# A hybrid diffusion backbone: the order of ScalarE's roots and copies in the modulation stage, and the place where the last modulation rows are stored

## The reference

```python
for i in range(DEPTH):                       # 2 layers
    mod_l = split(silu(c) @ ada_w[i] + ada_b[i], 6)       # for the latent tokens
    mod_c = split(silu(c_ctx) @ ada_w[i] + ada_b[i], 6)   # for the context tokens
    hl = rmsnorm(xl, norm_g[i, 0]) * (1 + sc1) + sh1
    hc = rmsnorm(xc, norm_g[i, 0]) * (1 + csc1) + csh1
    # layer 0: neighbourhood attention (q, k, v of 16 heads); layer 1: recurrent block
    xl = xl + gt1 * mixer_l;  xc = xc + cgt1 * mixer_c
    xl, xc = ... + gate2 * hier_moe(modulated rmsnorm of each)
out = rmsnorm(xl, final_g)
```

## Time and profile before

| | |
|---|---|
| median of 3 runs | 3079.86 us |
| lowest, highest | 3075.73, 3080.54 us |
| profiled execution | 3072.01 us |
| its span, first to last instruction | 3070.2 us |
| TensorE matmul busy | 2621.4 us (85%) |
| ScalarE, VectorE, GpSimd busy | 929.2, 1092.5, 420.1 us |
| mean granted TensorE clock | 0.929 |
| modulation stage | 0 to 197 us |

### The profile page before, as it was taken

One profiled execution on the slowest core, in us unless ns is written; L12 is line 12 of the kernel. 1 busy time (PEld: TensorE's weight loads), 2 busy tenths in 40 slices (PEclk: granted clock), 3 DMA queues, 4 the chain that ended last, 5 costly groups with the idle time before them and its releaser, 6 DMA issues. The chain is left out here.

```text
span 3070.2 us, 68426 instructions
## 1 busy us (share of the span) xinstructions
PE 2621.4 (85%) x27112; PEld 1748.1 (57%) x27113; DVE 1092.5 (36%) x2328; ACT 929.2 (30%) x2036; POOL 420.1 (14%) x628
## 2 busy tenths in 40 slices
PE   5779999999969959999999169999869599999980
PEld 1457777777735546666666134444335466666650
DVE  3423333333334432222222755556543322222226
ACT  1124434344430013333333214333400133333332
POOL 1110000000002012222222400000011122222223
PEclk8889999999989979999999579999979699999995
DMA  9741111111143277999999640000042689999986
GB/s 332 313 158 48 43 56 52 49 45 50 54 129 103 82 300 300 415 412 404 418 417 370 224 111 28 27 27 27 0 167 96 251 353 412 407 418 417 417 338 227
DMA packets 159129, 652.38 MB, mean 212 GB/s; under 512 B 42944, under 2 KB 57280, under 8 KB 103712
## 3 DMA queue, kind: packets, MB, share of 16 engines
q1 hardware_dynamic: 125648, 544.64, 45.5%
q10 hardware_dynamic: 15408, 55.59, 4.6%
q0 software_dynamic: 17952, 50.55, 4.6%
HBM read 575.65 MB, written 75.07 MB: 212 GB/s over the span
## 5 line engine op out<-in xcount | busy, mean ns | idle before, releaser
L1169 PE MATMUL PS<-wt,xT 128*32 128x256 f32 x13056 | 752.9, 381 | 55.9 <-issue 27.9
L1169 PEld LDWEIGHTS PS<-wt,xT 128*32 128x32 f32 x13056 | 504.2, 110 | 274.6 <-issue 79.3
L1109 ACT ACTIVATE y<-PS 32x256 f32<-32x256 f32 x832 | 312.6, 376 | 304.1 <-PE PS L1184 292.2
L1184 PE MATMUL PS<-wt,hidT 128*32 128x256 f32 x6528 | 396.3, 380 | 3.5 <-ACT y L1109 3.5
L740 PE MATMUL PS<-hT,slab 128*128 128x256 f32 x1680 | 384.9, 382 | 0.5
L1322 DVE STREAM_TRANSPOSE xT<-xg 128x256 f32<-128x256 f32 x210 | 93.5, 445 | 706.1 <-PE PS L1169 686.0
L740 PEld LDWEIGHTS PS<-hT,slab 128*128 128x128 f32 x1680 | 312.0, 191 | 45.3 <-issue 4.8
L1184 PEld LDWEIGHTS PS<-wt,hidT 128*32 128x32 f32 x6528 | 256.2, 110 | 101.5 <-issue 6.1
L1074 POOL DMA_INDIRECT xg<-h_d,ib x216 | 212.9, 986 | 174.8 <-POOL ib L1071 174.8
L1103 ACT ACTIVATE th<-PS 128x128 f32<-128x128 f32 x210 | 58.6, 279 | 524.5 <-PE PS L1169 519.3
L675 DVE TENSOR_REDUCE low<-PS 128x1 f32<-128x256 f32 x160 | 66.2, 422 | 378.9 <-PE PS L721 307.8
(11 more groups left out here) (252 smaller groups left out, 2610.6 us busy)
## 6 DMA issues: line engine op xcount, KB each, us to landing
wt<-in_w SPq DMA_DIRECT2D x256, 1024.0 KB, 22.8
wt<-in_w2s SPq DMA_DIRECT2D x128, 1024.0 KB, 25.1
OT<-in_ada_w SPq DMA_DIRECT2D x30, 1024.0 KB, 10.7
ys_d<-y ACTq DMA_DIRECT2D x52, 512.0 KB, 7.8
ys_d<-zero SPq DMA_DIRECT2D x8, 2368.0 KB
aw<-in_ada_w SPq DMA_DIRECT2D x18, 1024.0 KB, 10.4
slab<-in_qkv_s SPq DMA_DIRECT2D x24, 512.0 KB
x_d<-x_p ACTq DMA_DIRECT2D x18, 512.0 KB, 3.4
```

The source lines that it names most:

```text
L1109: ins = a.activation(buf[STRIP * j:STRIP * (j + 1), g * QD:(g + 1) * QD], PS[32 * g:32 * g + 32, DOWN, 0:QD], ACT.Copy)
L1169: mm = t.matmul(PS[32 * g:32 * g + 32, UP, 0:QD], xT[:, k * 32:k * 32 + 32], wt[b][:, q, c * 1024 + g * QD:c * 1024 + g * QD + QD], start= ...
L1184: mm = t.matmul(PS[32 * g:32 * g + 32, DOWN, 0:QD], hT[:, k * 32:k * 32 + 32], wt[b][:, q, c * 1024 + g * QD:c * 1024 + g * QD + QD], star ...
```

## The change

In ScalarE's list the two copies of column c now stand ahead of the roots of column c+1. For columns 1 to 3 the roots follow right behind the copies; for column 0 they follow behind the four pieces. (The roots of tiles 0 and 1 stay ahead of all.) GpSimd no longer stores the last of the six groups in the modulation. The tiles `mo` are allocated with what both stages share, and the attention's GpSimd list stores that group between the tables of pair 0 and those of pair 1.

```diff
-            return slab, qT, kT, VT, V, bq, mask, sl_in, sem("w_ps"), sem("w_used"), m_out
+            mo = [sbuf(stack, f"mo{j}", [P, CW4]) for j in range(2)]
+            return slab, qT, kT, VT, V, bq, mask, sl_in, sem("w_ps"), sem("w_used"), m_out, mo
+
+        def store_group(g, n, mo, m_out):
+
+            for j in range(QT):
+                g.dma_start(mod_d[:, n * GC + j * CW4:n * GC + (j + 1) * CW4],
+                            mo[n % 2][32 * j:32 * j + 2, :]).then_inc(m_out[n % 2], 16)
...
-                mo = [sbuf(st, f"mo{j}", [P, CW4]) for j in range(2)]
...
                         def store(n):
                             g.wait_ge(m_ready, QT * (n + 1))
-                            for j in range(QT):
-                                g.dma_start(mod_d[:, n * GC + j * CW4:n * GC + (j + 1) * CW4],
-                                            mo[n % 2][32 * j:32 * j + 2, :]).then_inc(m_out[n % 2], 16)
+                            store_group(g, n, mo, m_out)
...
-                        for n in range(NG):
+                        for n in range(NG - 1):
                             store(n)
                             if n + 2 < NG:
                                 load_bias(n + 2)
...
                         for c in range(NT // 2):
                             for n in (2 * c, 2 * c + 1):
-                                if n + 2 < NT:
-                                    root_(n + 2)
-                            for n in (2 * c, 2 * c + 1):
                                 evac(n)
+                            if 0 < c < NT // 2 - 1:
+                                root_(2 * c + 2)
+                                root_(2 * c + 3)
                             for i, (_, _, what, pc) in enumerate(FIRST):
                                 if pc == c:
                                     piece(i, what, c)
+                            if c == 0:
+                                root_(2)
+                                root_(3)
...
                         for h in range(2):
                             for j in range(2):
                                 table(h, h, j, True)
+                            if h == 0:
+                                store_group(g, NG - 1, mo, m_out)
```

More of the change, by code:

```diff
@@ L171, in modulation @@
         def modulation(hT, first, room):
-            slab, qT, kT, VT, V, bq, mask, sl_in, w_ps, w_used, m_out = first
+            slab, qT, kT, VT, V, bq, mask, sl_in, w_ps, w_used, m_out, mo = first
             with ExitStack() as st:
@@ L517, in attention @@
         def attention(hT, OT, first):
-            slab, qT0, kT0, VT, V0, bq, mask, sl_in, w_ps, w_used, m_out = first
+            slab, qT0, kT0, VT, V0, bq, mask, sl_in, w_ps, w_used, m_out, mo = first
             with ExitStack() as st:
```

## The result

The changed kernel took 3040.8 us (median; 3038.7 to 3044.0), the kernel before, on the same chip, 3078.8 (3075.7 to 3080.5). The ratio is 0.9879, with a 95% interval of 0.9861 to 0.9896: 38.0 us less. Forecast were 34.0 us less and 3045.9.

The account below looks back on a forecast made before the run. TensorE was taken to stand still for ScalarE's copies behind roots, with DMA engines full up to 104 us. TensorE's end 27.2 plus barrier 6.8 gave 34.0 us: 3079.9 to 3045.9, range 3037 to 3056.

Parts of the forecast that it names:

- the likeliest case: Whole kernel: 34.0 us less, 3045.9 us, own range 3041 to 3051, chance 0.67.
- ScalarE's order is what held TensorE: Modulation: roots ahead of copies make TensorE wait for `hT`; the wait falls from 30.2 us to about 1.5.
- Column 0 and 1: Modulation: column 0's V piece can start at 49.9 instead of 62.87, column 1's turns at 74.3 instead of 82.50.
- Column 2: Modulation: turns at 97.8, as load (2,7) may land at 96.9 instead of 94.4; by TensorE alone 96.5.
- The pace: Modulation: 19.8 us between columns with neither gap nor slow clock; from column 3 to 4 it had been 30.14.
- TensorE's end: End of the modulation: TensorE ends at 159.9 instead of 187.04, 27.2 us sooner.
- the low clock a case of its own: Rival: slow V pieces in columns 2 to 4 give back 8.6 us; 25.4 gained, 3054.5; chance 0.08.
- The weights: Second half of the modulation: weights in by 155, last load needed at 159, so TensorE's work limits by 4 us.
- The barrier: Modulation to attention: without the last store GpSimd's drain is short and the barrier opens with VectorE, 6.8 us gained.
- Its low end: Barrier: only 2.1 us gained if GpSimd's drain took its 5.3 us anyway; no chance of its own given.
- The moved stores: Attention: 2.06 us of GpSimd between the tables, covered by pair 1's 2.41 us wait for their load; cost 0.
- the first scores: Start of the attention: first scores near 163 us, 34 us sooner than 197.

Follow-up runs that it names:

- e1: Kernel before with only ScalarE's new order of roots and copies, the last store left in the modulation: 3051.3 us, ratio 0.9911.
- e6: Changed kernel with column 0's roots right behind its copies, ahead of its four pieces: 3039.7 us, one execution.
- e3: Changed kernel with the roots of tiles 2 and 3 again ahead of column 0's copies: 3051.7 us, ratio 0.9907.
- e12: Changed kernel unedited, run again beside two other timed kernels: 3043.5 us, ratio 0.989.
- e10: Changed kernel with column 0's roots behind its copies and ahead of its pieces, once more and timed: 3043.5 us, ratio 0.9892.
- e7: Changed kernel with 7 of 8 matmuls left out of the Q pieces of columns 3 and 4: TensorE's end 158.66, time 3057.5 us, one execution.
- e2: Changed kernel with ScalarE's old order, so only the last group's store is moved into the attention: 3072.8 us, ratio 0.9981.
- e8: Changed kernel with pair 0's tables loaded and made by GpSimd at the end of the modulation: 3049.4 us, ratio 0.9903.
- e4: Changed kernel unedited, run again on the same chip: 3044.0 us, ratio 0.9889.
- e11: Kernel before with ScalarE's new order alone, GpSimd also waiting for all its stores to land before the modulation's barrier: 3050.1 us, one execution.
- e5: Changed kernel with the last group stored inside the modulation again, by SyncE instead of GpSimd: 3051.6 us, one execution.

## Why the prediction was right

The mechanism held at each step that carried the time; one assumption, on GpSimd's drain, was wrong and cost nothing. The total was 5.1 us off: 3040.8 where 3045.9 was forecast, inside the range, and 0.2 us below the likeliest case's own range. The 5.1 us are two errors of opposite sign. The profiled execution came out 2.2 us slower than forecast (3040.15 against 3038.0). And the 7.9 us by which the median before lay above its profile were carried over to the median after, which lay only 0.7 us above its own: 7.2 us too many. That second term hangs on which execution the profiler happened to catch and says nothing of the mechanism; that it was partly made up for by the first is luck.

- **ScalarE's order is what held TensorE.** Right: the wait for `hT` went from 30.2 to 1.1 us (about 1.5 said), and e1 shows that the order alone does it.
- **Column 0 and 1.** The turns of column 1 were said to come at 74.3 and came at 71.6, with the token loads going out later and (2,0) landing sooner (26.0 us after its issue instead of 29.1). With the loads earlier they came at 75.3 (e6). The forecast had left the landing where it was. Column 2 turned at 97.2 to 98.4 either way.
- **Column 2** was said to turn at 97.8, by the loads and not by TensorE. It did, at 97.4, 98.4 and 97.2. The load ahead of it was waited for until 95.6, 96.6 and 96.2, between the two values that the prediction chose from (94.4 and 96.9), in two of three nearer to the later one that it took.
- **The pace.** Said: 19.8. Measured 19.80 in e3 three times over, in e12, and from column 3 to 4 in the changed kernel. From 2 to 3 it was 21.5 in its first profile, because of the low clock.
- **TensorE's end.** Said: 159.9, 27.2 us gained. Measured 161.16, and 161.78 and 159.26. This is the term that was off, by 1.3 us in the first profile. I gave the low clock a case of its own, with all V pieces of the later columns slow (8.6 us). What came was milder for the end: from 104 to 150 us the clock was 1.00, and only the stretch around column 2's turns, in two profiles of three, reached TensorE's end. But the low clock was less rare than the prediction had it. Its argument was the stretch from 7 to 34 us at a clock of 1.00; the same stretch ran at 0.70 in e6 and 0.64 in e10, the one behind it (34 to 46 us) at 0.50 in the changed kernel, and the one from 60 to 76 us at 0.79. All of these lie where the weights are the limit, and column 2 turned on time all the same.
- **The weights.** Said: TensorE the limit by 4 us. e7 shows 2.5 to 2.9.
- **The barrier.** Said: 6.8 us. Measured 6.80, by the change and by e2. But one assumption beneath it was wrong: that GpSimd's drain is next to nothing without a store just ahead. It takes 7.7 us. It is harmless because group 4's store is out by 151.8, early enough: the drain ends 5.4 us before VectorE's, which opens the barrier. Had it ended more than that later, it would have shown, and e8 shows that: work put on GpSimd at the end of the modulation brought the drain back onto the path. The 0.04 to 0.05 us that I went by the earlier trace rows were from barriers that stand right behind another one, where GpSimd had only cleared semaphores. The trace of before held a case much nearer to the one that I needed, drains of 8.9 us at the end of a list that waits for its DMAs (L1028, shown above), if of gathers; the prediction did not use it. Its low end, 2.1 us gained, was the right rival in kind; the distance of the last store from the barrier decided against it.
- **The moved stores.** Right: covered by the wait of the next tables for their load.

Said for the first scores: 163 us, 34.0 sooner. Measured 164.39, 32.67 sooner; the span shows 31.8, as the later stages took 0.9 us more (2874.0 against 2873.1). The medians differ by 38.0. Of the 6 us between the two measures no run shows that they are an effect of the change: the profiled execution of before lay 7 us below its median. Profiles of one kernel differ as much in their later stages: e12 had its scores 2.5 us sooner than e4 and a span 3.6 us longer (3041.8 and 3038.2); what took the time there was not traced.

Open: why GpSimd's drain ends 6.8 us behind its last DMA issue when that issue falls where the DMA engines are full (151.84 to 158.67), and 4.2 to 4.5 us behind its last instruction otherwise; and what it does in that time.

## What to carry to other kernels

An in-order engine with two kinds of work, one that others wait for and one that waits for late data, should have the first kind ahead; its price is read from the idle time of the engine that it feeds, with the slow clock behind each gap counted too. Before such a stall is priced, see whether the transfers are full beside it: in the first 104 us here a gap of 13 us was worth 5 at most. And before a barrier, take GpSimd's last DMAs out of the list or make them early, since its drain took 4.5 us here even with everything landed. To price a drain, look for one in the trace whose list did the same kind of work, not for the shortest.

## What the runs showed of the hardware

GpSimd's drain at the end of a list in which it had issued DMAs took 5.3 us right behind four stores, 4.5 with all of them landed (e11), 7.7 when the last stores were issued beside full DMA engines (the changed kernel), 8.9 behind gathers that the list waits for (L1028), and ended 4.2 us after the last table that GpSimd made (e8). In a list with tables and no DMA it ended 0.07 us behind the last table (L554). SyncE's own took 0.2 us behind four stores (e5).

Near 95 us, TensorE's granted clock fell to 1.2 GHz in the six profiles whose longest wait for a load there was 2.14 to 2.75 us, and held in the five where it was 0.21 to 1.85 us; at 67 us it fell after waits of 1.42 and 1.46 us. In the first profile of the changed kernel the fall near 95 us cost 1.7 us of one column's pace (97.44 to 118.92, 21.5 us instead of 19.8).
